# Norm statistics as four rows of 128 columns, in a three-block transformer kernel on one core

## The reference

```python
def rms_norm(t, w):
    tf = t.astype(jnp.float32)
    y = tf * lax.rsqrt(jnp.mean(tf * tf, axis=-1, keepdims=True) + NORM_EPS)
    return (y * w.astype(jnp.float32)).astype(t.dtype)

def modulate(h, shift, scale):
    return h * (1.0 + scale[:, None, :]) + shift[:, None, :]

# per layer, in the first block (norms 0 to 3)
h = modulate(rms_norm(x, mix_norm[layer]), sh1, sc1)
x = x + g1[:, None, :] * mixer(h)
h = modulate(rms_norm(x, ffn_norm[layer]), sh2, sc2)
x = x + g2[:, None, :] * swiglu(h, ffn_w1[layer], ffn_w2[layer])
```

## Time and profile before

| what | us |
|---|---|
| median of 3 runs | 3887.3 |
| lowest and highest | 3886.72, 3887.96 |
| the profiled execution, its own time | 3882.61 |
| its span, first to last instruction | 3881.0 |
| PE busy in it | 3437.4 |
| DVE busy | 2033.0 |
| ACT busy | 1189.3 |
| mean granted clock of PE | 0.942 |

### The profile page before, as it was taken

The page is one execution under the profiler, slowest core; times in us unless marked ns, Lnnn a source line. Parts: engine busy times, 40 slices in busy tenths (PEclk is TensorE's granted clock), DMA queues, the critical chain, the costliest instruction groups (busy, mean ns, idle before and its releaser), DMA issues. The chain is left out here.

```text
span 3881.0 us, 37630 instructions
## 1 busy us (share of the span) xinstructions
PE 3437.4 (89%) x13270; PEld 2504.3 (65%) x13270; DVE 2033.0 (52%) x2739; ACT 1189.3 (31%) x1517; POOL 112.0 (3%) x204
## 2 busy tenths in 40 slices
PE   4998689998689999976999999799997959998998
PEld 1444468886468877733788844578875725766886
DVE  5757455626448854335566269566533343336523
ACT  2221343324532213322444210344324222223221
POOL 0000000100000000000000030000000000000000
PEclk9997899999899999977999999899998979999999
DMA  5332145632025532200233311122332201222332
GB/s 214 108 120 66 42 133 191 198 116 65 22 76 195 192 117 80 92 17 22 76 97 95 95 54 49 55 81 93 97 108 76 87 11 71 92 70 81 97 98 70
DMA packets 100417, 361.00 MB, mean 93 GB/s; under 512 B 11152, under 2 KB 11168, under 8 KB 100064
## 3 DMA queue, kind: packets, MB, share of 16 engines
q1 hardware_dynamic: 77936, 276.07, 21.9%
q0 software_dynamic: 20080, 75.27, 5.9%
q10 hardware_dynamic: 2304, 8.39, 0.6%
HBM read 357.59 MB, written 2.10 MB: 93 GB/s over the span
## 5 line engine op out<-in xcount | busy, mean ns | idle before, releaser
L1718 DVE TENSOR_TENSOR weight_lo<-weight_ring,weight_hi 128x1024 fp32r<-128x1024 f32 (+1 forms) x462 | 556.6, 1207 | 1060.6 <-ACT weight_hi L1176 1056.3
L1176 ACT ACTIVATE weight_hi<-weight_ring 128x1024 fp32r<-128x1024 f32 (+1 forms) x462 | 482.3, 1046 | 1508.0 <-PE proj_banks L719 1148.6
L719 PE MATMUL proj_banks<-h_lo,weight_hi 128*128 128x512 f32 x1776 | 692.2, 390 | 0.0
L719 PE MATMUL proj_banks<-h_hi,weight_hi 128*128 128x512 f32 x1344 | 523.9, 390 | 8.8 <-DVE weight_lo L1718 8.8
L719 PE MATMUL proj_banks<-h_hi,weight_lo 128*128 128x512 f32 x1344 | 523.4, 389 | 0.0
L719 PEld LDWEIGHTS proj_banks<-h_lo,weight_hi 128*128 128x128 f32 x1776 | 334.2, 188 | 69.2
L719 PE MATMUL proj_banks<-mid_lo,weight_hi 128*128 128x512 f32 x768 | 300.1, 391 | 0.0
L719 PEld LDWEIGHTS proj_banks<-h_hi,weight_hi 128*128 128x128 f32 x1344 | 252.6, 188 | 62.8 <-issue 10.4
L719 PEld LDWEIGHTS proj_banks<-h_hi,weight_lo 128*128 128x128 f32 x1344 | 252.7, 188 | 52.7
L719 PE MATMUL proj_banks<-mid_hi,weight_hi 128*128 128x512 f32 x704 | 275.2, 391 | 7.3 <-DVE weight_lo L1718 7.3
L719 PE MATMUL proj_banks<-mid_hi,weight_lo 128*128 128x512 f32 x704 | 274.9, 390 | 0.0
(11 more groups left out here) (317 smaller groups left out, 5081.3 us busy)
## 6 DMA issues: line engine op xcount, KB each, us to landing
weight_ring<-in_w_up SPq DMA_DIRECT2D x176, 512.0 KB, 3.5
ada_ring<-in_ada POOLq DMA_DIRECT2D x96, 512.0 KB, 3.8
weight_ring<-in_w_dn SPq DMA_DIRECT2D x64, 512.0 KB, 3.5
weight_ring<-in_w_br SPq DMA_DIRECT2D x32, 512.0 KB, 3.6
weight_ring<-in_w_upr SPq DMA_DIRECT2D x32, 512.0 KB, 3.5
weight_ring<-in_w_dnr SPq DMA_DIRECT2D x32, 512.0 KB, 3.5
scratch<-in_ada POOLq DMA_DIRECT2D x24, 512.0 KB, 4.3
weight_ring<-in_w_dn SPq DMA_DIRECT2D x32, 384.0 KB, 3.1
```

What stands on the lines that cost most here:

```text
L719: last = mm(proj.banks[:, u % RING, :], stationary(split0 + n)[:, w], moving(k), start=k + m == 0, stop=k == kt - 1 and m == 2)
L1176: return nc.scalar.activation(out, in_, func, **kw)
L1718: return v.tensor_tensor(out, a, b, op)
```

## The change

It touches all eleven norms, `first_pair` and `residual`:

- DVE adds squares 1 to 6 onto square 0 (`sum_up`). In the eight norms that follow a `residual` this stands in `residual` at k = 7, ahead of the wait for the last output tile; in norms 0, 9 and 10 it stands at the head of DVE's norm.
- PE takes eight matmuls of 128 columns instead of eight of 512: for each block j of 128 tokens the squares (first the sum of seven, then square 7) move past four columns, "pick", of which column j is one. The result is 4x128, one row for each block.
- ACT takes the root of 4x128 and DVE the reciprocal of 4x128. PE then spreads each row over 128 partitions with four matmuls of "sel" into one more bank, ("bc", r), and DVE reads it from there.
- DVE multiplies by the gain and the spread statistic in one instruction. In split modulated norms ACT adds the shift and rounds in one instruction, and the low part is made from H(k), the shift and the rounded part. ACT takes a root of one column of eps behind the seventh square. The second of the two weight chunks that are rounded within a norm moves behind the root on ACT and behind the reciprocal on DVE.
- `first_pair` runs its low part with k outside and the two tiles inside, so that it waits for each H(k) in turn.
- The last four rows of the next layer's modulation, its bias and its gains move into the first five steps of `residual` of dn0 and dn1.

```diff
@@ -100,6 +100,7 @@
+        "pick": np.tile(np.eye(4).reshape(1, 16), (P, 1)),
...
@@ -226,26 +227,27 @@
         k += [("cum", h - 1, j) for j in range(NB)] if 1 <= h <= 4 else []
         k += [("sb", h - 2)] if h >= 2 else []
...
@@ -678,12 +681,12 @@
-        for t in range(2):
-            for k in range(KD):
-                if t == 0:
-                    pe.wait_ge(s["h_ready"], h_count(r, k))
+        for k in range(KD):
+            pe.wait_ge(s["h_ready"], h_count(r, k))
+            for t in range(2):
                 last = mm(proj.bank((name, t)), c.hi(split0 + t)[:, k * P:(k + 1) * P], lo(k), start=False, stop=k == KD - 1)
-            last.then_inc(proj.full_sem, 1)
+                if k == KD - 1:
+                    last.then_inc(proj.full_sem, 1)
 
@@ -782,7 +785,19 @@
         last.then_inc(mix.full_sem, 1)
 
     def norm(r):
-        sum_squares(("ss", r), lambda k: (s["sq_ready"], 8 * r + k + 1), lambda k: T(squares_at(r) + k), KD)
+
+        bank = open_bank(mix, ("ss", r))[0:4, 0:P]
+        for half, (sem, n) in enumerate(((s["sq_summed"], 6 * (r + 1)), (s["sq_ready"], 8 * (r + 1)))):
+            pe.wait_ge(sem, n)
+            squares = T(squares_at(r) + (KD - 1 if half else 0))
+            for j in range(NB):
+                last = mm(bank, c.const("pick")[:, 4 * j:4 * j + 4], squares[:, j * P:(j + 1) * P], start=half + j == 0, stop=half + j == NB)
+        last.then_inc(mix.full_sem, 1)
+        bank = open_bank(mix, ("bc", r))
+        pe.wait_ge(s["rstd_ready"], r + 1)
+        for j in range(NB):
+            last = mm(bank[:, j * P:(j + 1) * P], c.const("sel")[0:4, j * P:(j + 1) * P], T(RSTD)[0:4, P:2 * P], start=True, stop=True)
+        last.then_inc(mix.full_sem, 1)
...
@@ -1230,21 +1244,25 @@
             else:
                 act.wait_ge(s["x_ready"], 8 * (r - 9) + k + 1)
             st.done(f(T(squares_at(r) + k), X(k), ACT.Square), s["sq_ready"])
-            if r in SPLIT_UP and k == KD - 2:
-
-                up = SPLIT_UP[r]
-                for n in range(SPLIT_RING):
-                    round_chunk(up, n)
-        root(("ss", r), T(RSTD), D)
+            if k == KD - 2:
+
+                st.link(f(c.small[:, 160:161], eps, ACT.Sqrt))
+                if r in SPLIT_UP:
+                    round_chunk(SPLIT_UP[r], 0)
+        act.wait_ge(*mix.filled(("ss", r)))
+        ins = f(T(RSTD)[0:4, 0:P], mix.bank(("ss", r))[0:4, 0:P], ACT.Sqrt, scale=1.0 / D, bias=eps[0:4, :])
+        ins.then_inc(mix.emptied(("ss", r))[0], 1)
+        if r in SPLIT_UP:
+            round_chunk(SPLIT_UP[r], 1)
         if r in MODULATED:
             use, layer, part, ready = MODULATED[r]
             act.wait_ge(s["mod_ready"], ready)
             for k in range(KD):
                 act.wait_ge(s["xn_ready"], 8 * list(MODULATED).index(r) + k + 1)
-                ins = f(H(k), H(k), ACT.Identity, scale=c.g(use, k), bias=c.m(layer, part, k))
-                ins.then_inc(s["h_raw"] if r in SPLIT_NORMS else s["h_ready"], 1)
                 if r in SPLIT_NORMS:
-                    round_h(r, k)
+                    st.done(f(c.norm_hi(r, k), H(k), ACT.Identity, bias=c.m(layer, part, k)), s["h_rounded"])
+                else:
+                    f(H(k), H(k), ACT.Identity, bias=c.m(layer, part, k)).then_inc(s["h_ready"], 1)
         elif r in SPLIT_NORMS:
...
@@ -1751,29 +1769,49 @@
         dve.wait_ge(*mix.emptied(key))
         st.link(v.reciprocal(rt, rt))
 
+    def sum_up(r, k):
+
+        total = T(squares_at(r))
+        dve.wait_ge(s["sq_ready"], 8 * r + k + 1)
+        st.done(tt(total, total, T(squares_at(r) + k), ALU.add), s["sq_summed"])
+
     def norm(r):
+        if r not in NORM_AFTER:
+            for k in range(1, KD - 1):
+                sum_up(r, k)
         if r in SPLIT_UP:
-            for n in range(SPLIT_RING):
-                rest_chunk(SPLIT_UP[r], n)
-        inverse(("ss", r), T(RSTD))
+            rest_chunk(SPLIT_UP[r], 0)
+        dve.wait_ge(*mix.emptied(("ss", r)))
+        st.done(v.reciprocal(T(RSTD)[0:4, P:2 * P], T(RSTD)[0:4, 0:P]), s["rstd_ready"])
+        if r in SPLIT_UP:
+            rest_chunk(SPLIT_UP[r], 1)
+        dve.wait_ge(*mix.filled(("bc", r)))
+        rstd = mix.bank(("bc", r))
         for k in range(KD):
             if r in MODULATED:
-                st.done(tt(H(k), X(k), T(RSTD), ALU.mult), s["xn_ready"])
+                st.done(stt(H(k), X(k), c.g(MODULATED[r][0], k), rstd, ALU.mult, ALU.mult), s["xn_ready"])
             else:
                 name, at = PLAIN[r]
                 out = X(k) if r == 8 else H(k)
-                ins = stt(out, X(k), c.v(name, at + k), T(RSTD), ALU.mult, ALU.mult)
+                ins = stt(out, X(k), c.v(name, at + k), rstd, ALU.mult, ALU.mult)
                 if r == 8:
                     st.done(ins, s["x_ready"])
                 elif r in SPLIT_NORMS:
-                    ins.then_inc(s["h_raw"], 1)
+                    st.done(ins, s["h_raw"])
                 else:
                     ins.then_inc(s["h_ready"], 1)
                     dve.wait_ge(s["h_ready"], h_count(r, k))
+        dve.sem_inc(*mix_release(mix, ("bc", r)))
         if r in SPLIT_NORMS:
             for k in range(KD):
                 dve.wait_ge(s["h_rounded"], 8 * SPLIT_NORMS.index(r) + k + 1)
-                tt(c.norm_lo(r, k), H(k), c.norm_hi(r, k).bitcast(F32), ALU.subtract).then_inc(s["h_ready"], 1)
+                hi = c.norm_hi(r, k).bitcast(F32)
+                if r in MODULATED:
+                    use, layer, part, _ = MODULATED[r]
+                    ins = stt(c.norm_lo(r, k), H(k), c.m(layer, part, k), hi, ALU.add, ALU.subtract)
+                else:
+                    ins = tt(c.norm_lo(r, k), H(k), hi, ALU.subtract)
+                ins.then_inc(s["h_ready"], 1)
                 dve.wait_ge(s["h_ready"], h_count(r, k))
 
     def rest_chunk(name, n):
@@ -1797,13 +1835,17 @@
         dve.wait_ge(s["mid_rounded"], i * 2 + n)
         tt(lo, raw, hi.bitcast(F32), ALU.subtract).then_inc(s["mid_ready"], 1)
 
-    def residual(stage, gate=None, bias=None):
-
+    def residual(stage, gate=None, bias=None, after=None):
+
+        r = [r for r in NORM_AFTER if NORM_AFTER[r] == stage][0]
         for k in range(KD):
             key, per = (stage, k), len(pieces(STAGE[stage][3]))
             if per > 1:
                 for n in range(per * k + SPLIT_RING, min(per * (k + 1) + SPLIT_RING, per * KD)):
                     rest_chunk(stage, n)
+            if k == KD - 1:
+                for done in range(1, KD - 1):
+                    sum_up(r, done)
             dve.wait_ge(*proj.filled(key))
             if gate is not None:
                 ins = stt(X(k), proj.bank(key), gate(k), X(k), ALU.mult, ALU.add)
@@ -1812,6 +1854,8 @@
+            if after is not None:
+                after(k)
...
+    def last_row(layer, ctx, j):
+
+        row = 48 * layer + j - len(FIRST_ROWS)
+        if ctx:
+            dve.wait_ge(*c.ada_has_landed(row))
+            st.link(v.tensor_tensor_reduce(T(54, 2), c.ada_slot(row), c.cond[:, D:2 * D], 1.0, 0.0, ALU.mult, ALU.add, c.mod[:, 3 * 48 + j:3 * 48 + j + 1]))
+        ada_row(row, c.cond[:, 0:D], c.mod[:, 48 * layer + j:48 * layer + j + 1])
+
+    def rest_of_modulation_1(k):
+
+        if k < 4:
+            last_row(1, False, 44 + k)
+        elif k == 4:
+            add_bias(1, 0, 48, "ada_b", 48)
+            gains(2, 1, 1, "mix_norm", 8)
+            gains(3, 1, 4, "ffn_norm", 8)
+
+    def rest_of_modulation_2(k):
+
+        if k < 4:
+            last_row(2, True, 44 + k)
+        elif k == 4:
+            add_bias(2, 0, 48, "b_mod_3", 0)
+            add_bias(3, 0, 48, "b_mod_3", 0)
+            gains(6, 3, 1, "g_pre_mix_3", 0)
+            gains(4, 2, 1, "g_pre_mix_3", 0)
+            gains(5, 2, 4, "g_pre_mlp_3", 0)
+            st.link(tt(c.g(7, 0, 8), c.m(2, 2, 0, 8), c.v("g_post_mix_3", 0, 8), ALU.mult))
+            st.link(tt(c.g(8, 0, 8), c.m(2, 5, 0, 8), c.v("g_post_mlp_3", 0, 8), ALU.mult))
 
...
-    add_bias(1, 0, 48, "ada_b", 48)
-    gains(2, 1, 1, "mix_norm", 8)
-    gains(3, 1, 4, "ffn_norm", 8)
-    residual("dn0", gate=lambda k: c.m(0, 5, k))
+    residual("dn0", gate=lambda k: c.m(0, 5, k), after=rest_of_modulation_1)
...
```

More of the change, by code:

```diff
@@ L210, in mixing_keys @@
 def mixing_keys():
-    k = [("ss", 0)]
+    k = [("ss", 0), ("bc", 0)]
     k += [("rot_i", t) for t in range(5)]
@@ L228, in mixing_keys @@
         k += [("av", *units[n - 2])] if n >= 2 else []
-    k += [("ss", 1), ("ss", 2)]
+    k += [("ss", 1), ("bc", 1), ("ss", 2), ("bc", 2)]
     k += [("stat_s", t) for t in range(8)] + [("pool", g) for g in range(4)]
@@ L234, in mixing_keys @@
         k += [("sb", h - 2)] if h >= 2 else []
-    k += [("ss", 3), ("ss", 4)]
+    k += [("ss", 3), ("bc", 3), ("ss", 4), ("bc", 4)]
     k += [("acol", 0)]
@@ L241, in mixing_keys @@
         k += [("mn", h, 0), ("mn", h, 1), ("md", h), ("stat_m", h)]
```

(28 more changed lines are left out.)

2 lines of the change are left out of this document (1 added, 1 removed).

## The result

The changed kernel takes 3908.8 us (median of 5 runs, 3898.7 to 3910.9), the kernel before 3887.7 (5 runs). The ratio is 1.0047, with a 95% interval of 1.0032 to 1.0061. The forecast was 3843, range 3820 to 3862. The time missed by 66 us and in the wrong direction.

A forecast was written before the change was run, and what follows sets the result against it. PE was taken as the bound in most stages, with time to win where it stands still. Terms sum to 45.0 us: 3882.61 - 45.0 = 3837.6, plus 4.7 for the median, 3842.3, rounded to 3843; range 3820 to 3862.

The forecast's parts named there:

- rival E: Clock stays at 1.2 GHz for the whole first pair, 7.1 us more at each of nine restarts, 64; 3907, chance 0.03.
- norms 8 and 9: Net gain of 2.5 us taken, bounds 0 and 6; norm 9 puts a reciprocal wait into PE ahead of "ck".
- norm 0: Nothing covers DVE's six additions there, so PE restarts at 71.4 instead of 66.42: 5.0 us lost.
- moved rows: Modulation rows moved between residuals remove PE's wait for DVE's first weight part ahead of dn1: 6.7 us gained, bounds 4 and 6.75.
- norm 10: Uncovered additions make PE's restart 1.3 us late; with the first pair's 2.0 and 1.7, 1.0 us lost.
- Chain of the statistics: Norms 1 to 3, last square to PE's restart: 5.9 us against 13.08, 7.2 less, counted as 7.1.
- Rival B: Short matmuls run cold at 2.0 us a group, two groups at ten norms, 12 us more; 3855, chance 0.11.
- First pair: High matmuls after the restart in modulated norms take 9.6 us against 11.62, 2.0 less.
- Rival A: Clock doesn't fall in the shorter gap before PE's restart, 2.0 us more gained at nine restarts; 3825, chance 0.17.
- Low part with k outside: In the first pair the first bank fills later, so the next tile's weights come later: 1.7 us lost at seven first pairs.
- Rival C: Weights become the bound: PE waits for DVE's weight part after first pairs; 3860, or near 3872 if most; chance 0.05.
- Residual's cover, tables (F and D): F: additions uncovered in residuals, 34 us, about 3882, chance 0.04; D: table loads at ten norms, 25.6, 3869, chance 0.02.

The follow-up runs named there:

- r4_after_plus_128: The changed kernel with small widened by another 32 unused columns (128 bytes), so h and mid tiles lie at a multiple of 256; 3835.7 us, ratio 0.9869.
- r1_after_old_addresses: The changed kernel with its two table additions in a tensor at the end of SBUF, every other tensor at its old address; 3836.2 us, ratio 0.9870.
- r3_norms_0_9_10_old: r1_after_old_addresses with the old statistics (eight products of ones, 128x512 root and reciprocal, no additions) at norms 0, 9 and 10 only; 3818.0 us, ratio 0.9819.
- r2_h_at_64: r1_after_old_addresses with 64 unused bytes a partition ahead of h_tiles, the weights staying at a multiple of 256; 3867.2 us, ratio 0.9949.

## Why the prediction was wrong, step by step

**The step that failed** is one that the prediction does not have. It went through the instructions and gave no term to the two tables that grow, though the diff shows them. Two wider tables do no work themselves, but they moved the activation tiles of some 10,600 split matmuls by 128 bytes against their weights. The prediction took the pace of these matmuls as given; it went from 226.7 to 232.7 ns. That cost 61 us in the profiled execution and 69 in the medians (3905.2 against 3836.2). No rival spoke of the matmuls' own pace in the steady stages; the slower rival E was about the clock, and the clock is not it: granted 0.939 after, 0.942 before, 1.00 in both windows, and 0.939 at the old addresses too, where the kernel is fast.

**The sum of the terms held, in part by luck.** 45.0 us were forecast. With the addresses restored the profiled execution is 3882.6 - 3837.9 = 44.7 shorter, the medians by 50.8. That the profiled execution comes so near is luck: in the table the stretches of dn1 and mout gave 10 us more than was said, those of abo, dn0 and norms 8 and 9 some 10 less. Stretch by stretch, at DVE's first addition to x in each projection (start us, from the two traces):

| x of | before | old addresses | gained | forecast |
|---|---|---|---|---|
| abo | 461.22 | 469.11 | -7.9 | -5.0 (norm 0) |
| dn0 | 775.28 | 780.02 | 3.2 | 7.4 (norm 1) |
| cdo | 1087.03 | 1085.80 | 6.0 | 7.4 (norm 2) |
| dn1 | 1412.32 | 1392.12 | 19.0 | 14.1 (norm 3, moved rows) |
| mout | 1835.56 | 1805.69 | 9.7 | 4.8 (norm 4) |
| dn2 | 2146.56 | 2111.75 | 4.9 | 3.5 (norm 5) |
| cout | 2478.07 | 2435.94 | 7.3 | 6.5 (norm 6) |
| dn3 | 2788.51 | 2743.01 | 3.4 | 4.8 (norm 7) |
| norm 10's | 3484.39 | 3438.92 | 0.0 | 2.5 (norms 8, 9) |
| output | 3867.23 | 3822.50 | -0.7 | -1.0 (norm 10) |

A stretch alone is good to a few us: the kernel before, run again, was 4.5 us later at abo, where the granted clock falls and rises many times. And r4_after_plus_128, as fast as r1_after_old_addresses, gains 8.0 us at dn0, norm 1, where the table has 3.2.

- **Chain of the statistics**: right, 5.44 against 5.9. The short groups cost 1.04 and 1.12 us at the full clock, where 1.4 was taken. Rival B happened in part. In the changed kernel's trace the spreading group runs at half the clock, in 2.04 us, at norms 6, 8 and 9 (at norm 6 the line below, granted 0.50), and at norm 1 of r1_after_old_addresses, where from the start of the second short group to the restart it is 6.31 us and not 5.39. At the other norms it takes 1.12 to 1.37. The 12 us of B count both groups at the low clock at ten norms.

```profile
2249.01 2.04 PE L799 MATMUL mix_banks<-scratch,others 4*128 4x128 f32 x8 [1.64 <-DVE scratch L1785]
```

- **First pair**: the high pass takes 8.85 us in the changed kernel (511.94 to 520.79), forecast 9.6. In r1_after_old_addresses the low clock lasted longer and it took 10.3. Rival A did not happen at norm 1: the clock still fell (granted 0.53 at 512 to 515).
- **Low part with k outside**: right in sign and about in size, -16 against -12. Rival C's sign shows in the same place: the wait for weight_lo behind it grew from 2.05 to 3.64.
- **Moved rows**: right sign, under-sized: 12.4 by the medians, 8.7 in the stretch of dn1 alone, against 6.7 and a stated bound of 6.75.
- **Norm 0**: forecast 5.0. PE restarts 6.4 us later (72.78 against 66.42). Of this 0.85 is there before the norm, since the last gain ends at 60.43 and not at 59.58. The six additions take 4.32 as said, and all sixteen "pick" records come behind them, in 3.24 us, with a pace near that of norm 9 at half the clock (3.57):

```profile
64.93 3.24 PE L794 MATMUL mix_banks<-scratch,others 128*4 128x128 f32 x16 [64.93 <-DVE scratch L1736]
69.82 1.12 PE L799 MATMUL mix_banks<-scratch,others 4*128 4x128 f32 x8 [1.65 <-DVE scratch L1785]
72.78 1.19 PE L668 MATMUL proj_banks<-h_tiles,weight_ring 128*128 128x512 f32 x1 [1.84 <-ACT h_tiles L1191]
```

- **Norms 8 and 9**: forecast +2.5, measured 0. With the old statistics at norm 9 the stretch is 6.8 us shorter, so that norm 8 gained about 7 and norm 9 lost it again, most of it by the clock (see r3_norms_0_9_10_old). The bounds "0 and 6" hid this by adding the two.
- **Norm 10**: near, -0.7 against -1.0 by the table; the old statistics there gave back 3.3.
- **Residual's cover, tables (F and D)**: neither happened at norm 1, by the rows above; the additions end 0.53 us ahead of residual 7, and no load follows the square.

## What to carry to other kernels

A diff that changes the size of any tensor in SBUF changes the address of all behind it: list the addresses of the moving and stationary tiles before and after, modulo 256 bytes, as one lists instructions. Put small additions at the end of the allocation, or pad them to 256; both gave the fast spacing here. And when a time differs, compare the count of matmuls in a window where PE is busy throughout before looking at waits: 432 against 443 told here in one line what all the waits could not. A trick that trades one engine's work for another's belongs only where the other has cover; by the stretches of the table it paid at norms 1 to 8, and taking it back at 0, 9 and 10 gave 18 us.

## What the runs showed of the hardware

- The spacing of back-to-back 128x512 fp32r matmuls depends on the distance in SBUF between the moving and the stationary tile. At the old distance and at 256 bytes more (0 modulo 256) it is 226.7 ns. With the tiles 128 bytes off it is 232.4 ns in most stages and 233.3 in some, 232.5 to 232.7 as the mean of the loops. At -64 it is 233.3. At +64 it is 228.9 to 229.1, but 233.3 in the last down projection of r2_h_at_64, so that the distance is not all that counts. Only these four distances were tried, and only this pattern of a kernel in which every matmul loads other weights. fp32 matmuls kept 429 to 430 ns from record to record at all four distances.
- The slow spacings are patterns that repeat for hundreds of matmuls, such as 229, 237, 229, 238 in one stage of the changed kernel. Which pattern a stage takes differs between executions, and with it the mean: the last up projection of the second block has 232.4 ns in one trace of the changed kernel and 233.3 in the other. The mechanism stays open.
- The Trainium skill, "TensorE: Matmul & The Clock Gate", in "Wait — 56ns, not 53.3ns?", gives 215.7 ns from start to start for 512 columns once warm, and names no address. Split products stay 11 ns above it even at the best distance here, and the measurement decides. The 429 to 430 ns of a record of an fp32 matmul are near twice the page's figure; what a record does in that time no run here shows.
